# First feed-forward layer: seven products for eight in 1792 of 2816 rows of the down projection, and other places for the weight-quarter loads

## The chip, the cores and the metric

The kernel runs on one core of a Trainium2 chip. TensorE (PE) multiplies, VectorE (DVE) and ScalarE (ACT) evacuate, round and add, GpSimd (POOL) does small work and issues the DMAs that add into their destination, and SyncE (SP) issues the other DMAs. The metric is the device time of one execution in microseconds.

## The reference, cut to what matters

Two transformer-like blocks follow each other on x of 512 tokens by 1024 channels. The change lies in the feed-forward layer of the first block; a part of it touches that of the second.

```python
D_FF = 2816
# first block
h = rms_norm(x, pre_ffn_norm[l])
f = (jax.nn.silu(h @ w_gate[l]) * (h @ w_up[l])) @ w_down[l]   # w_down: 2816 x 1024
x = x + rms_norm(f, post_ffn_norm[l])
...
# end of the second block
h = rmsnorm(x, norm_ffn[i])
x = x + jnp.square(jax.nn.relu(h @ w_up[i])) @ w_down[i]       # w_down_2: 4096 x 1024
return rmsnorm(x, norm_final)
```

## The kernel before, in words

**Arithmetic.** Every float32 matrix product is done as three products of rounded parts: each operand is split into a high part (`hi`, `hH`, `aH`, `fH`: an ACT copy into a rounded type) and the rest (`lo`, `hL`, `aL`, `fL`: a DVE subtraction), and PE adds high by high, high by low and low by high in one PSUM bank. A matmul has 128 rows of weights and moves 512 columns (256 in the blocks of kind `half`).

**Units, slots, blocks.** Weights come in units of 256 rows by 512 columns (512 KB). SP loads a unit into one of three buffers `raw` (`load_unit`), ACT rounds it into one of six `hi` buffers, DVE writes the rest into `lo` (`split_weights` on both). The list `BLOCKS` fixes the order: for the first feed-forward layer `gu0` to `gu10` (each makes 256 of the 2816 hidden columns, gate and up) with the down projection in three pieces between them: `dn00`, `dn01` after `gu2` (768 rows), `dn10`, `dn11` after `gu6` (1024 rows), `dn20`, `dn21` after `gu10` (1024 rows). PE's program is a list of numbered slots, mostly of 6 matmuls of 512 columns or 12 of 256. Every engine's program is written slot by slot from the same tables (`CONV_AT` for conversions, `TR_AT` for transposes, `DONE_AT` for evacuations, `FS_*_AT` for the seven products), but no engine waits for a slot: it runs through its own list in order and waits on semaphores alone. What stands ahead in an engine's list therefore holds up everything behind it.

**Start of a layer.** `gu0` and `up0` (first block of the second layer) are of kind `half`: 16 slots, first for tokens 0 to 255, then from slot 8 on for tokens 256 to 511. Meanwhile the normalised tiles of the later tokens are still transposed: PE turns tile `i` (into banks `s`, semaphore `s_ntr`), ACT rounds it (`norm_round`, `hH<-s`), DVE makes the rest (`norm_rest`, `hL<-s`, semaphore `s_nlo`). In `gu0` the last two turns (i = 14 and 15) stand in slots 6 and 7, ACT's roundings of them in its slots 7 and 8, and PE's slot 8 waits until `s_nlo` shows 15. ACT's conversion of the second unit of `gu1` stands in slot 6, ahead of both roundings. In `up0` the last turn (the 44th) stands in slot 5. The conversions of the four units of the next block stand in slots 2, 6, 10 and 14, and the evacuations of the block itself (ACT, then DVE) behind them, in slots 15 and 16; the next block's first slot waits for the first of these evacuations.

**Seven products.** The second layer's down projection already goes in four rounds `fs0` to `fs3`, each with 1024 rows, as a 2 by 2 by 2 product of parts in seven products for eight. Per round SP loads one quarter each into the buffers `a`, `b`, `c`, `d` (`wq`, for `a` the two buffers `hn`), two DMAs of 512 KB for each (`load_quarter`), and POOL adds further quarters to them by adding DMAs (`later_quarters`), so that the sums of weights cost no engine. The sums of the hidden part are DVE's (`sum_hidden`), and each is rounded and split (`round_hidden`, `rest_hidden`). The 28 slots of a round take 14 conversions of weights, 14 evacuations, 8 roundings and 8 rests. `WQ_BEFORE` says ahead of which unit SP issues a quarter: for `fs0` ahead of its own first four units, which need no `raw` load, so behind all loads of `up1`. The quarters of `fs0` wait for `s_ntr` 44, since they overwrite `hn`.

```python
def load_quarter(f, i):                                        # L800, before
    w, j, n = (("d", 1, 1), ("b", 0, 1), ("a", 0, 0), ("c", 1, 0))[i]
    u0 = BLK["fs0"].u0 if f == 0 else BLK[f"fs{f - 1}"].u0
    for x in range(2):
        if f == 0:
            o.wait_ge(s_ntr, 44)
```

Of the kernel before, what the change touches and what calls it, by code (L numbers as in the profile page):

```python
# [15 lines left out]
S = 512  # L16
# [82 lines left out]
def blocks():  # L99
# [89 lines left out]
def conversions():  # L189
# [239 lines left out]
FS_D_AT = when([s0(f"fs{f}") + s for f in range(NFF2) for s in (-30, -24, -22, -2, -1, 2)])  # L429
FS_S_AT = when([s0(f"fs{f}") + s for f in range(NFF2) for s in (-14, 1, 2, 3)])  # L430
# [43 lines left out]
def build(nc, A, out, scr):  # L474
    ctx = ExitStack()
    with ctx:
# [37 lines left out]
        s_fhi, s_flo, HID = s_ahi, s_alo, 2 * sum(nb for _, nb in FF1)  # L514
# [32 lines left out]
        s_wd, WD_FROM = s_os, 64  # L547
# [119 lines left out]
        WQ = [x[:, :].rearrange("p (k n) -> p k n", k=2) for x in HN] + [sb(f"wq{i}", [128, 2, 512], c=P8)[:, :, :] for i in range(6)]  # L667
# [5 lines left out]
        def fa(i, j):  # L673

            return FA[j - 1][:, :, 256 * i - 256:256 * i]


        def landed(f, w, n):
# [3 lines left out]
            return s_wd[WQ_I[w] // 2], WD_FROM + 32 * ((WQ_PER[w] - 1) * f + n - 1)  # L682
# [4 lines left out]
        def sync_program(e):  # L687
# [6 lines left out]
            def load_gain(i):  # L694
# [9 lines left out]
                if i in (5, 7):  # L704
                    o.wait_ge(s_xup, {5: 8, 7: 16}[i])
# [18 lines left out]
            def load_unit(b, u):  # L724
# [75 lines left out]
            def load_quarter(f, i):  # L800

                w, j, n = (("d", 1, 1), ("b", 0, 1), ("a", 0, 0), ("c", 1, 0))[i]
                u0 = BLK["fs0"].u0 if f == 0 else BLK[f"fs{f - 1}"].u0
                for x in range(2):
                    if f == 0:

# [4 lines left out]
                    e.dma_start(WQ[WQ_I[w] + x], rows(A["w_down_2"][0], 4 * f + 2 * j + x, 512 * n, 512 * n + 512)).then_inc(s_wq[WQ_I[w] // 2], 16)  # L811
# [34 lines left out]
        def scalar_program(e):  # L846
# [48 lines left out]
            def split_weights(j):  # L895

                f = [f for f in range(NFF2) if 0 <= j - BLK[f"fs{f}"].u0 < 14]
                if f:
# [53 lines left out]
            def evacuate(b, i):  # L952
# [19 lines left out]
                elif n[:2] == "gu":  # L972
                    g = int(n[2:])

                    if g:
# [4 lines left out]
                elif n[:2] == "dn":  # L980

                    o.wait_ge(s_xup, 8)
                    h = int(n[3])
                    e.activation(Y[:, i, 512 * h:512 * h + 512], bank[:, :], ACT.Copy).then_inc(s_eva, 1)
                elif n[:2] == "ex":
                    j = int(n[2])

                    o.wait_ge(s_os[i], 16 * j)
# [30 lines left out]
                elif n[:2] == "up":  # L1019
                    k = int(n[2])  # L1020

                    if k >= 2:
                        o.wait_ge(s_flo, HID + 8 * (k // 2))
                    e.activation(FA[k % 2][:, i, :], bank[:, :], ACT.Relu).then_inc(s_rl, 1)

            def round_products(b, i):

                n = b.name
                if n[:2] == "gu" and i >= 2:
                    g = int(n[2:])  # L1030
                    o.wait_ge(s_evd, EVACUATED[b.e0 + i][1])
                    c = [b0 for b0, _ in FF1 if b0 <= g][-1]

                    if c:
                        x = BLK[f"dn{[b0 for b0, _ in FF1].index(c) - 1}1"]
                        o.wait_ge(s_bank, x.e0 + 4)
                    e.activation(aH[:, 2 * (g - c) + i - 2, :], SG[i - 2][:, :], ACT.Copy).then_inc(s_ahi, 1)
# [127 lines left out]
            def convolutions(g):  # L1165
                for i in CV_AT.get(g, ()):
# [4 lines left out]
                    o.wait_ge(s_xsv, 16)  # L1171
# [1464 lines left out]
```

## Time and profile before

| | us |
|---|---|
| median of 3 runs | 1813.27 (1813.20 to 1813.41) |
| the profiled execution | 1813.32 |
| its span | 1811.5 |
| PE busy | 1776.8 (98%) |
| DVE busy | 1114.1 (62%) |
| ACT busy | 834.3 (46%) |
| POOL busy | 336.4 (19%) |

The span is the execution without 1.8 us at its ends. PE's busy time is that of its records, which overlap: a matmul of 512 columns is shown with 0.39 us, while the next one starts 0.23 us later. How much PE really gets done is seen better from the number of matmuls in a stretch. Times inside the program are microseconds from the start of the span. The first layer's part that is changed runs from about 222 to 585 us, the second feed-forward layer from about 1474 us to the end.

### The profile page before, as it was taken

How to read it: one execution, taken by the hardware profiler on the slowest of the kernel's cores; microseconds unless marked ns; L12 is line 12 of the kernel's file. 1: busy time of each engine (PE TensorE's matmuls, PEld its weight loads, DVE VectorE, ACT ScalarE, POOL GpSimd, SP SyncE). 2: the span in 40 equal slices, each digit the busy share in tenths (PEclk: the TensorE clock that was granted, in tenths of full speed). 3: DMA queues.
4: the chain of work that ended last, by engine and by line, in shares of the span. 5: the costliest groups of instructions: out<-in, count | busy, mean ns of one | idle time of the engine just before them, and what ended most of it. 6: DMA issues, size and time to landing. Idle time of an engine off the chain costs nothing.

```text
span 1811.5 us, 24680 instructions
## 1 busy us (share of the span) xinstructions
PE 1776.8 (98%) x9586; PEld 1449.5 (80%) x9586; DVE 1114.1 (62%) x1763; ACT 834.3 (46%) x1593; POOL 336.4 (19%) x404
## 2 busy tenths in 40 slices
PE   7999999999999999999999999999999999999998
PEld 7767898888888877878878787767788998888886
DVE  7556643233345787887768746677556357574847
ACT  5346532222224555554555644554434445352535
POOL 1403000000000046254462640000020012112120
PEclk9999999999999999999999999999999999999999
DMA  7212333332322453352433444233443248849482
GB/s 256 72 58 63 101 110 116 93 93 93 94 93 75 152 143 128 119 149 97 160 131 123 142 147 164 86 105 118 139 151 130 69 148 189 236 101 259 117 206 70
DMA packets 140419, 230.85 MB, mean 127 GB/s; under 512 B 27264, under 2 KB 59456, under 8 KB 139664
## 3 DMA queue, kind: packets, MB, share of 16 engines
q1 hardware_dynamic: 118944, 166.70, 29.0%
q0 software_dynamic: 20496, 60.10, 12.5%
q10 hardware_dynamic: 864, 2.49, 0.3%
q8 instruction: 76, 1.25, 0.3%
q14 instruction: 39, 0.32, 0.1%
HBM read 216.54 MB, written 12.71 MB: 127 GB/s over the span
## 4 chain that ended last, share of the span: by engine, by line
PE 80%; DVE 11%; ACT 3%; DMA 3%; issue 2%; POOL 1%; SPq 0%; DVEq 0%; ACTq 0%; POOLq 0%
PE m L2135 14%; PE m L2137 13%; PE m L2136 13%; PE m L2146 6%; PE m L2148 6%; PE m L2147 6%; PE s L2298 4%; DVE lo L1396 3%; DMA raw<-in_w_up_dram 2%; PE m L2245 2%; PE m L2244 2%; PE m L2243 2%; PE s L2294 1%; PE m L2270 1%; PE m L2272 1%
## 5 line engine op out<-in xcount | busy, mean ns | idle before, releaser
L2135 PE MATMUL m<-hH,hi 128*128 128x512 f32 (+1 forms) x1392 | 529.4, 380 | 3.2 <-DVE hL L1426 1.8
L2137 PE MATMUL m<-hH,lo 128*128 128x512 f32 (+1 forms) x1392 | 509.1, 366 | 0.0
L2136 PE MATMUL m<-hL,hi 128*128 128x512 f32 (+1 forms) x1392 | 508.3, 365 | 0.0
L1396 DVE TENSOR_TENSOR lo<-raw,hi 128x1024 fp32r<-128x1024 f32 x267 | 335.8, 1269 | 189.7 <-ACT hi L916 189.4
L916 ACT ACTIVATE hi<-raw 128x1024 fp32r<-128x1024 f32 x267 | 276.1, 1050 | 200.8 <-DMA raw<-in_w_up_dram 52.9
L2135 PEld LDWEIGHTS m<-hH,hi 128*128 128x128 f32 x1392 | 262.6, 189 | 47.7 <-DVE hL L1426 2.4
L2137 PEld LDWEIGHTS m<-hH,lo 128*128 128x128 f32 x1392 | 262.4, 189 | 43.4
L2136 PEld LDWEIGHTS m<-hL,hi 128*128 128x128 f32 x1392 | 262.9, 189 | 39.0
L2146 PE MATMUL m<-hi,hH 128*128 128x512 f32 (+1 forms) x320 | 133.8, 418 | 1.6 <-DVE lo L1396 1.6
L2148 PE MATMUL m<-hi,hL 128*128 128x512 f32 (+1 forms) x320 | 122.5, 383 | 0.0
L2147 PE MATMUL m<-lo,hH 128*128 128x512 f32 (+1 forms) x320 | 122.4, 382 | 0.0
L1463 DVE TENSOR_TENSOR sg<-sg,m 128x512 f32<-128x512 f32 x44 | 29.8, 685 | 116.1 <-ACT sg L979 111.3
L2243 PE MATMUL m<-hi,fH 128*128 128x512 f32 x224 | 87.1, 389 | 0.0
L2244 PE MATMUL m<-lo,fH 128*128 128x512 f32 x224 | 87.1, 389 | 0.0
L2245 PE MATMUL m<-hi,fL 128*128 128x512 f32 x224 | 87.1, 389 | 0.0
L1226 ACT ACTIVATE X<-hn,BIAS 128x128 f32<-128x128 f32 x256 | 80.7, 391 | 4.4 <-POOL hn L2015 4.3
L2077 POOL DMA_DIRECT2D scr_x_dram<-X x1 | 0.5, 542 | 414.1 <-DVE X L1447 414.1
L2060 POOL DMA_DIRECT2D wq<-in_w_down_dram x32 | 39.2, 1645 | 184.2 <-DMA wq<-in_w_down_dram 111.2
L2146 PEld LDWEIGHTS m<-hi,hH 128*128 128x128 f32 x320 | 60.5, 189 | 13.6 <-DVE lo L1396 2.1
L2148 PEld LDWEIGHTS m<-hi,hL 128*128 128x128 f32 x320 | 60.5, 189 | 12.3
L905 ACT ACTIVATE hi<-wq 128x1024 fp32r<-128x1024 f32 x40 | 42.1, 1054 | 58.2 <-PE m L2137 40.6
L2146 PE MATMUL m<-hi,aH 128*128 128x512 f32 x176 | 68.9, 391 | 0.0
(330 smaller groups left out, 3032.6 us busy)
## 6 DMA issues: line engine op xcount, KB each, us to landing
raw<-in_w_in_dram SPq DMA_DIRECT2D x72, 512.0 KB, 3.6
wq<-in_w_down_dram POOLq DMA_DIRECT2D x40, 512.0 KB, 10.0
hn<-scr_cs_dram POOLq DMA_DIRECT2D x32, 512.0 KB, 4.1
raw<-in_w_up_dram SPq DMA_DIRECT2D x32, 512.0 KB, 5.7
wq<-in_w_down_dram SPq DMA_DIRECT2D x24, 512.0 KB, 7.7
raw<-in_w_gate_dram SPq DMA_DIRECT2D x44, 256.0 KB, 2.8
raw<-in_w_up_dram SPq DMA_DIRECT2D x44, 256.0 KB, 3.1
raw<-in_w_down_dram SPq DMA_DIRECT2D x22, 512.0 KB, 4.2
```

The source lines that it names most:

```text
L916: e.activation(d, r, ACT.Copy).then_inc(s_hi, 1)
L1226: x = e.activation(to[:, h % 2, k], HN[h % 2][:, 512 * d + 128 * c:512 * d + 128 * c + 128], ACT.Exp, bias=BIAS[:, c, 32 * d + h:32 * d + ...
L1396: e.tensor_tensor(d, r, h.bitcast(F32), ALU.subtract).then_inc(s_lo, 1)
L2135: e.matmul(bank, wh[:, kk, c], h[:, k, q], start=k == 0, stop=False)
L2136: e.matmul(bank, wh[:, kk, c], l[:, k, q], start=False, stop=False)
L2137: x = e.matmul(bank, wl[:, kk, c], h[:, k, q], start=False, stop=k == kt - 1)
L2146: e.matmul(bank, h[:, k, q], wh[:, kk, c], start=k == 0, stop=False)
L2147: e.matmul(bank, h[:, k, q], wl[:, kk, c], start=False, stop=False)
L2148: x = e.matmul(bank, l[:, k, q], wh[:, kk, c], start=False, stop=k == kt - 1)
L2243: e.matmul(m[:, :], fH[n % 4][:, k, q], wh[:, kk, :], start=k == 0 and p in FS_FRESH, stop=False, skip_group_check=True)
L2244: e.matmul(m[:, :], fH[n % 4][:, k, q], wl[:, kk, :], start=False, stop=False, skip_group_check=True)
L2245: y = e.matmul(m[:, :], fL[n % 4][:, k, q], wh[:, kk, :], start=False, stop=k == 3, skip_group_check=True)
```

## The change

- The down projection's first 768 rows (`ds0`, after `gu2`) and the next 1024 (`ds1`, after `gu6`) are done in seven products, as in the second layer; the last 1024 rows stay as they were (`dn20`, `dn21`). In `ds0` each half of the rows has 3 blocks of 128, so every second slot has 3 matmuls instead of 6. `dn00`, `dn01`, `dn10`, `dn11` are gone. The number of slots stays 1106; the units grow from 323 to 337.
- DVE writes the product of gate and up for `gu0` to `gu6` into `fa1` buffers; ACT and DVE don't split it there any more. The products of `ds0`, `ds1` are evacuated by DVE into `Y`, by a multiplication by 1 or -1 the first time.
- The buffers for the quarters are `hn` (a), the four rows of `X` (b, c), `gain0` and a new buffer `wqf` (d). So `X` is saved to `scr_x` by a 2 MB DMA of POOL when its first update is done, and brought back near the end of `ds1`. Two gain vectors are loaded later (ahead of `gu8` instead of `gu2`).
- SP issues the quarters of `ds0` ahead of units of `gu1` and `gu2`, those of `ds1` ahead of units of `gu4`, `gu5`. They wait for `s_ntr` 16, `s_hn` 16 and `s_mlo` 8, b and c also for the saved `X`.
- For the second layer the quarters of `fs0` now stand ahead of the second, third and fourth unit of `up1` and of the first of `fs0`; those of `fs1` to `fs3` are spread over more units too. POOL's adding DMAs have new slots.

```diff
-FF1 = [(0, 3), (3, 4), (7, 4)]
+FF1 = 7
 NFF2 = 4
+SEVEN = ["ds0", "ds1"] + [f"fs{f}" for f in range(NFF2)]
...
+    for b in range(11):
+        add(f"gu{b}", "fm" if b else "half", 4, "dddd")
+        if b in (2, 6):
+            add(f"ds{b // 4}", "fs", 14, "d" * 14)
+    for h in range(2):
+        add(f"dn2{h}", "tmt" if h else "tm", 4, "dddd")
...
-WQ_BEFORE = {BLK[f"up{2 * f}"].u0 + u: (f, i) for f in range(NFF2) for i, u in enumerate((3, 4, 5, 6) if f else (8, 9, 10, 11))}
+SEVEN_K = [3, 4] + [4] * NFF2
+SEVEN_ROW = [0, 768] + [1024 * f for f in range(NFF2)]
+WQ_AFTER = [[("gu1", 1), ("gu2", 0), ("gu1", 3), ("gu2", 2)], [("gu4", 0), ("gu4", 2), ("gu5", 0), ("gu5", 2)], [("up1", 1), ("up1", 2), ("up1", 3), ("fs0", 0)]]
...
+def unit_tiles(f, x):
+    return SEVEN_K[f] - 2 if x else 2
...
             def load_quarter(f, i):
                 w, j, n = (("d", 1, 1), ("b", 0, 1), ("a", 0, 0), ("c", 1, 0))[i]
...
                     if f == 0:
+                        o.wait_ge(s_ntr, 16)
+                        o.wait_ge(s_hn, 16)
+                        o.wait_ge(s_mlo, 8)
+                        if w in ("b", "c"):
+                            o.wait_ge(s_xsv, 16)
+                    elif f == 2:
                         o.wait_ge(s_ntr, 44)
...
+                    d = s[:, :]
+                    if i >= 2 and g < FF1:
...
+                        d = FA1[k // SEVEN_K[c]][:, k % SEVEN_K[c], :]
+                    e.tensor_tensor(d, s[:, :], bank[:, :], ALU.mult).then_inc(s_evd, 1)
...
+                    if first and not f:
+                        e.tensor_scalar(x, bank[:, :], -1.0 if i // 2 in FS_MINUS else 1.0, None, ALU.mult).then_inc(s_evd, 1)
...
+                if g == s0("gu1") + 2:
+                    o.wait_ge(s_xup, 8)
+                    e.dma_start(scr["x"], X[:, :, :].rearrange("p t d -> p (t d)")).then_inc(s_xsv, 16)
+                if g == s0("gu7") + 2:
+                    o.wait_ge(s_lo, BLK["ds1"].u0 + 12)
+                    e.dma_start(X[:, :, :].rearrange("p t d -> p (t d)"), scr["x"]).then_inc(s_xbk, 16)
...
-                    for kk in range(2):
+                    for kk in range(unit_tiles(n // 7, x)):
```

**SP's list at `gu1`, before.** The rows are the loads of the first, second and third unit of `gu1` (each a gate half and an up half), then those of the fourth with a gain vector:

```order
L741 DMA raw1<-in_w_up_dram 128x2x256
L740 DMA raw2<-in_w_gate_dram 128x2x256 [waits s_lo]
L741 DMA raw2<-in_w_up_dram 128x2x256
L740 DMA raw0<-in_w_gate_dram 128x2x256 [waits s_lo]
L741 DMA raw0<-in_w_up_dram 128x2x256
L740 DMA raw1<-in_w_gate_dram 128x2x256 [waits s_lo]
L741 DMA raw1<-in_w_up_dram 128x2x256
L740 DMA raw2<-in_w_gate_dram 128x2x256 [waits s_lo]
L741 DMA raw2<-in_w_up_dram 128x2x256
L722 DMA gain1<-in_post_ffn_norm_dram 128x1024 [waits s_xup]
```

The same place now; `raw2` is the first unit of `gu1`, `raw0` the second:

```order
L786 DMA raw2<-in_w_gate_dram 128x2x256 [waits s_lo]
L787 DMA raw2<-in_w_up_dram 128x2x256
L864 DMA gain0<-in_w_down_dram 128x2x512 [waits s_mlo,s_hn,s_ntr]
L864 DMA wqf<-in_w_down_dram 128x512
L786 DMA raw0<-in_w_gate_dram 128x2x256 [waits s_lo]
L787 DMA raw0<-in_w_up_dram 128x2x256
L786 DMA raw1<-in_w_gate_dram 128x2x256 [waits s_lo]
L787 DMA raw1<-in_w_up_dram 128x2x256
L864 DMA hn0<-in_w_down_dram 128x2x512
L864 DMA hn1<-in_w_down_dram 128x512
L786 DMA raw2<-in_w_gate_dram 128x2x256 [waits s_lo]
L787 DMA raw2<-in_w_up_dram 128x2x256
```

Quarter d now stands, with its three waits, between the first and the second unit of `gu1`, and quarter a ahead of the fourth.

**ACT's list in `gu0`, now** (the same instructions in the same order as before). `hi2` is the first unit of `gu1`, `hi3` the second, `hH<-s2` and `hH<-s3` are the roundings of tiles 14 and 15:

```order
L969 ACTIVATE hi2<-raw2 128x1024 [waits s_unit,s_raw2]
L1003 ACTIVATE hH<-s0 128x4x128 [waits s_ntr]
L1003 ACTIVATE hH<-s1 128x4x128 [waits s_ntr]
L969 ACTIVATE hi3<-raw0 128x1024 [waits s_raw0]
L1003 ACTIVATE hH<-s2 128x4x128 [waits s_ntr]
L1003 ACTIVATE hH<-s3 128x4x128 [waits s_ntr]
```

Nothing moved here: `hi3` still stands ahead of the last two roundings; what moved is the load that it waits for.

**SP's list at `up1`, before.** `raw2`, `raw0`, `raw1` ahead of `wq4` are the second to fourth unit of `up1`:

```order
L798 DMA raw1<-in_w_up_2_dram 128x2x512 [waits s_lo]
L798 DMA raw2<-in_w_up_2_dram 128x2x512 [waits s_lo]
L798 DMA raw0<-in_w_up_2_dram 128x2x512 [waits s_lo]
L798 DMA raw1<-in_w_up_2_dram 128x2x512 [waits s_lo]
L798 DMA raw2<-in_w_up_2_dram 128x2x512 [waits s_lo]
L811 DMA wq4<-in_w_down_2_dram 128x2x512 [waits s_ntr]
L811 DMA wq5<-in_w_down_2_dram 128x2x512
L811 DMA wq0<-in_w_down_2_dram 128x2x512
L811 DMA wq1<-in_w_down_2_dram 128x2x512
L811 DMA hn0<-in_w_down_2_dram 128x2x512
L811 DMA hn1<-in_w_down_2_dram 128x2x512
L811 DMA wq2<-in_w_down_2_dram 128x2x512
```

The same place now, from the first unit of `up1` on:

```order
L844 DMA raw1<-in_w_up_2_dram 128x2x512 [waits s_lo]
L864 DMA wq4<-in_w_down_2_dram 128x2x512 [waits s_ntr]
L864 DMA wq5<-in_w_down_2_dram 128x2x512
L844 DMA raw2<-in_w_up_2_dram 128x2x512 [waits s_lo]
L864 DMA wq0<-in_w_down_2_dram 128x2x512
L864 DMA wq1<-in_w_down_2_dram 128x2x512
L844 DMA raw0<-in_w_up_2_dram 128x2x512 [waits s_lo]
L864 DMA hn0<-in_w_down_2_dram 128x2x512
L864 DMA hn1<-in_w_down_2_dram 128x2x512
L844 DMA raw1<-in_w_up_2_dram 128x2x512 [waits s_lo]
L864 DMA wq2<-in_w_down_2_dram 128x2x512
L864 DMA wq3<-in_w_down_2_dram 128x2x512
```

The quarters moved ahead of three of the four loads of `up1`; counted from `wq4`, these are the third, sixth and ninth DMA.

## Rows read from the trace of the kernel before

**Rows 1.** Stretches: busy time and count of each engine, granted clock, DMA.
```profile
core 0: us, PE busy (x) PEld busy (x) DVE busy (x) ACT busy (x) POOL busy (x), PEclk, DMA share, GB/s
...
400.00:500.00 100.00, 100.00 (x443) 82.81 (x442) 36.13 (x42) 24.43 (x29) 0.00 (x0) 1.00 0.28 88
```

**Rows 2.** The same columns, one round of seven products (`fs1`).
```profile
1601.40:1639.50 38.10, 38.10 (x170) 31.55 (x169) 34.26 (x38) 19.84 (x21) 4.15 (x4) 1.00 0.42 106
```

**Rows 3.** SP in order of time, around `gu0`: start, duration, instruction.
```profile
221.36 0.37 SPq L740 DMA_DIRECT2D raw<-in_w_gate_dram  x1
221.77 0.76 SPq L741 DMA_DIRECT2D raw<-in_w_up_dram  x1
```

**Rows 4.** ACT in order of time, in `gu0`.
```profile
229.40 1.05 ACT L916 ACTIVATE hi<-raw 128x1024 fp32r<-128x1024 f32 x1
232.84 0.60 ACT L950 ACTIVATE hH<-s 128x512 fp32r<-128x512 f32 x1 [2.39 <-PE s L2298]
234.72 0.60 ACT L950 ACTIVATE hH<-s 128x512 fp32r<-128x512 f32 x1 [1.28 <-PE s L2298]
```

**Rows 5.** PE (first two) and DVE (last) in order of time, in `gu0`.
```profile
234.08 0.60 PE L2298 MATMUL s<-CST,hn 128*128 128x128 f32 x4
234.44 0.36 PE L2135 MATMUL m<-hH,hi 128*128 128x256 f32 x1
...
233.47 0.69 DVE L1426 TENSOR_TENSOR hL<-s,hH 128x512 fp32r<-128x512 f32 x1 [0.41 <-ACT hH L950]
```

**Rows 6.** SP in order of time, at `up0`.
```profile
1474.39 7.13 SPq L798 DMA_DIRECT2D raw<-in_w_up_dram  x3
1482.35 1.91 SPq L811 DMA_DIRECT2D wq<-in_w_down_dram  x4
```

**Rows 7.** Landing times of quarter DMAs issued together: the 1st; 2nd and 3rd; 7th and 8th.
```profile
DMA to landing us min/median/max: 5.1/5.1/5.1
...
DMA to landing us min/median/max: 6.7/7.0/7.3
...
DMA to landing us min/median/max: 11.7/13.4/15.0
```

**Rows 8.** SP (first) and POOL: issues of the last two quarters, first adding DMAs.
```profile
1486.28 1.54 SPq L811 DMA_DIRECT2D wq<-in_w_down_dram  x2
...
1489.77 2.54 POOL L2060 DMA_DIRECT2D wq<-in_w_down_dram  x2 [11.73 <-DMA wq<-in_w_down_dram]
```

**Rows 9.** ACT, DVE and PE in order of time, where `up0` ends and `up1` begins.
```profile
1492.49 1.06 ACT L916 ACTIVATE hi<-raw 128x1024 fp32r<-128x1024 f32 x1 [1.82 <-PE m L2137]
1496.03 2.76 ACT L1024 ACTIVATE fa<-m 128x512 f32<-128x512 f32 x4 [2.48 <-PE m L2137]
...
1496.73 1.41 DVE L1504 TENSOR_TENSOR fa<-fa,m 128x512 f32<-128x512 f32 x2 [4.80 <-PE m L2137]
...
1497.99 0.40 PE L2135 MATMUL m<-hH,hi 128*128 128x512 f32 x1
```

**Rows 10.** Landing time of two plain loads of the same queue, at `gu0` (gate and up).
```profile
DMA to landing us min/median/max: 2.7/2.7/2.7
...
DMA to landing us min/median/max: 3.0/3.2/3.3
```

**Rows 11.** Landing time of the 2 MB store of `X`, at `bc0`.
```profile
DMA to landing us min/median/max: 7.7/7.7/7.7
```

**Rows 12.** Stretches around the longest pause of PE; columns as in rows 1.
```profile
655.00:660.00 5.00, 2.29 (x23) 1.60 (x23) 4.90 (x5) 4.11 (x10) 4.04 (x6) 1.00 0.72 197
660.00:665.00 5.00, 5.00 (x18) 3.94 (x16) 4.89 (x6) 1.44 (x4) 0.56 (x1) 0.66 0.76 198
```

**Rows 13.** DVE in order of time in `fs1`: a sum, a rest, an evacuation.
```profile
1604.27 1.22 DVE L1551 SCALAR_TENSOR_TENSOR gain<-fa 128x1024 f32<-128x1024 f32 x1
...
1610.14 1.22 DVE L1535 TENSOR_TENSOR fL<-gain,fH 128x1024 fp32r<-128x1024 f32 x1
1611.27 0.68 DVE L1517 TENSOR_TENSOR X<-m,X 128x512 f32<-128x512 f32 x1
```

More of the change, by code:

```diff
@@ L513, in build @@
         s_gs, s_ahi, s_alo, s_rl = (sem(f"s_{n}") for n in ("gs", "ahi", "alo", "rl"))
-        s_fhi, s_flo, HID = s_ahi, s_alo, 2 * sum(nb for _, nb in FF1)
+        s_fhi, s_flo = s_ahi, s_alo
         s_cwt, s_cw, s_cid, s_tanh, s_silu = (sem(f"s_{n}") for n in ("cwt", "cw", "cid", "tanh", "silu"))
@@ L666, in build, with fa, sums, part @@
         fL = [sb(f"fL{i}", [128, 4, 256], F32R, c=P8) for i in range(4)]
-        WQ = [x[:, :].rearrange("p (k n) -> p k n", k=2) for x in HN] + [sb(f"wq{i}", [128, 2, 512], c=P8)[:, :, :] for i in range(6)]
+        WQ2 = [x[:, :].rearrange("p (k n) -> p k n", k=2) for x in HN] + [sb(f"wq{i}", [128, 2, 512], c=P8)[:, :, :] for i in range(6)]
         P8.close()
         FS2 = G[1][:, :].rearrange("p (k t) -> p k t", k=4)
-        def fa(i, j):
-            return FA[j - 1][:, :, 256 * i - 256:256 * i]
+        def fa(f, i, j):
+            return (FA if f >= 2 else FA1)[j - 1][:, 0:SEVEN_K[f], 256 * i - 256:256 * i]
+        def sums(f):
+            return FS2[:, 0:SEVEN_K[f], :]
+        def part(f, p):
+            return [fa(f, 1, 1), fa(f, 1, 2), sums(f), fa(f, 1, 1), fa(f, 2, 1), fa(f, 1, 2), fa(f, 2, 2)][p]
+        def split_part(n):
+            if n < 14:
+                return tuple(x[:, 2 * (n % 4):2 * (n % 4) + 2, :].rearrange("p a (b c) -> p (a b) c", b=2) for x in (aH, aL))
+            return fH[n % 4], fL[n % 4]
+        def wq(f, w, x):
+            return (WQ2 if f >= 2 else WQ0)[WQ_I[w] + x][:, 0:unit_tiles(f, x), :]
+        def quarter(f, j, c, x):
+            w = A["w_down_2"][0] if f >= 2 else A["w_down"][0]
+            r0 = SEVEN_ROW[f] + 128 * (SEVEN_K[f] * j + 2 * x)
+            return w[r0:r0 + 128 * unit_tiles(f, x), 512 * c:512 * c + 512].rearrange("(k p) n -> p k n", p=128)
         def landed(f, w, n):
@@ L703, in load_gain @@
                     o.wait_ge(s_sn, 4)
-                if i in (5, 7):
-                    o.wait_ge(s_xup, {5: 8, 7: 16}[i])
+                if i == 5:
+                    o.wait_ge(s_xup, 8)
+                    o.wait_ge(s_flo, rests(1) + 8)
+                if i == 6:
+                    o.wait_ge(s_lo, BLK["ds1"].u0 + 14)
+                if i == 7:
+                    o.wait_ge(s_xup, 16)
                 if i in (9, 10):
@@ L1028, in round_products @@
                 n = b.name
-                if n[:2] == "gu" and i >= 2:
+                if n[:2] == "gu" and int(n[2:]) >= FF1 and i >= 2:
                     g = int(n[2:])
                     o.wait_ge(s_evd, EVACUATED[b.e0 + i][1])
[L1032 to L1037, printed above, removed]
+                    o.wait_ge(s_bank, BLK["ds1"].e0 + 14)
+                    e.activation(aH[:, 2 * (g - FF1) + i - 2, :], SG[i - 2][:, :], ACT.Copy).then_inc(s_ahi, 1)
             def round_hidden(g):
@@ L1411, in norm_scale @@
                     o.wait_ge(s_ntr, 2 * n - 2)
+                if 8 <= n < 12:
+                    o.wait_ge(s_lo, BLK["ds1"].u0 + 8)
                 if n >= 12:
@@ L2233, in block @@
                     p, t, x = s // 4, s // 2 % 2, s % 2
-                    n, i, j = 7 * int(b.name[2]) + p, s // 2, b.u0 + 2 * p + x
-                    o.wait_ge(s_flo, HID + 8 * (n // 7) + (x + 2 if p == 1 else FS_LAST[p] + 1))
+                    n, i, j = 7 * SEVEN.index(b.name) + p, s // 2, b.u0 + 2 * p + x
+                    o.wait_ge(s_flo, rests(n // 7) + (x + 2 if p == 1 else FS_LAST[p] + 1))
+                    hh, hl = split_part(n)
+                    last = SEVEN_K[n // 7] - 1
                     wh, wl = weights(j)
```

179 lines of the change are left out of this document (95 added, 84 removed).

## The prediction

> **What bounds the kernel now.** The page first: PE is busy for 98% of the span, DVE for 62%. So I looked for what PE does per 100 us, in the view of stretches: 443 matmuls of 512 columns start in 100 us of the first layer [rows 1], which is 0.226 us each. In the round `fs1`, the pattern that the change copies, the stretch holds 170 matmul records (168 of its own and two cut at the ends) in 38.1 us, again 0.226 us each, and DVE is busy for 34.3 of the 38.1 us [rows 2]. So the seven products don't slow PE, though DVE has little left there. PE is the bound in both layers; what it is spared counts in full, and every wait that reaches it as well. Then I read SP, ACT, DVE and PE in order of time at the two places where SP's list changes: `gu0` [rows 3 to 5] and `up0` [rows 6 to 9].
>
> **What is removed.** Before: 14 blocks of 128 rows by 4 token tiles by 2 halves by 3 = 336 matmuls. Now: `ds0` has 7 products by 2 tiles by 3 blocks by 3 = 126, `ds1` 7 by 2 by 4 by 3 = 168, together 294. 42 matmuls go, at 0.226 us each [rows 1]: **-9.5 us**. The weights are loaded beside the matmuls as before. Bounds: -9.0 to -9.7, since nothing else of PE changes in these blocks.
>
> **The products beside DVE.** In `ds0` PE needs 126 by 0.226 = 28.5 us. DVE has from its start on, by its list: 14 evacuations and the last product of `gu2` at 0.60 (an operation of 0.68 overlaps its neighbour by 0.08), 7 rests and 3 sums at 0.87 (three quarters of the 1.22 of 1024 elements, less the overlap), 9 conversions of quarters, 5 of them short ones (0.60), 4 long (1.14), and 4 of `gu3` at 1.14: 9.0 + 8.7 + 3.0 + 4.6 + 4.6 = 29.9 us [rows 13]. That is 1.4 us more than PE, but the last two operations on this list are wanted only in `gu3`. The tightest point is the third product, at 8.2 us in `ds0`: by the same costs its rest is done at 7.2, a lead of 1 us. In `fs1` it is done 9.9 us after the start (1611.4 to 1601.4) and wanted at 10.9, the same lead, and PE loses nothing [rows 2, 13]. `ds1` has the sizes of `fs1`. I take **0** for both, bounds 0 and +4 (every product late by some tenths). The 14 additional conversions, the DMAs of POOL (its list is empty in this layer) and the two 2 MB copies of `X` lie beside PE. The store lands 7.7 us after its issue [rows 11], begins at about 226 and so is over before the quarters start.
>
> **Stall A, in `gu0`.** SP issued the load of the second unit of `gu1` at 221.36 [rows 3]; ACT converted it at 229.40, ahead of the roundings of tiles 14 and 15 at 232.84 and 234.72 [rows 4]. Now quarter d stands ahead of this load and waits for `s_ntr` 16, the last turn of PE, which starts at 234.08 and is seen by ACT at 234.72 [rows 4, 5]. So SP stands still from 221.4 to 234.7. Then it issues two DMAs for d (0.75 MB) and the two halves of the unit (0.5 MB). When do they land? Of quarters issued together the first lands after 5.1 us, the second 6.7 after its issue, the third 7.3 [rows 7], with 0.48 us between issues [rows 6]; counted from the first issue 5.1, 7.2 and 8.3 us for 0.5, 1.0 and 1.5 MB. For 1.25 MB that is 7.7 us: 242.4. Lower bound: the unit lands as if alone, 3.2 us after its own issue at 236.2 [rows 10], at 239.4; upper bound 8.3 us and 2 us more for other traffic, 245. I take the middle one, as a burst like that of rows 7 stands there. Then ACT converts (1.05), rounds tile 14 (0.6), DVE makes the rest (0.69) [rows 4, 5]: 244.7. PE's slot 8 needs this rest. Slot 7 begins at 234.44 and has 12 matmuls at 0.12, so slot 8 would begin at 235.9; before, the rest was there at 234.2 (233.47 and 0.69) [rows 5]. PE stands still for 244.7 - 235.9 = **8.8 us**, bounds 5.8 and 11.4. No other engine can give this back: PE was the bound, and tiles 14 and 15 wait behind the conversion whatever else is ready. This is the cover that is gone: between load and conversion lay 8 us, and the wait takes 13.
>
> **Stall B, at `up1`.** The same wait, `s_ntr` 44, now stands in front of the second unit of `up1`, and the quarters between its units. The roundings of the last turn are ahead of the conversion here, so `up0` itself is not held up. But the fourth unit, whose load was issued long before the quarters [rows 6], is now the ninth of a burst that begins at 1482.35. The seventh and eighth of that burst land at 1498.0 and 1502.2 (11.7 and 15.0 us after issues at 1486.3 and 1487.2) [rows 7, 8], the last ones slowed by the adding DMAs from 1489.77 on [rows 8]. A ninth at the pace of the earlier ones, 1 to 2 us apart, lands at about 1503.7; bounds 1497.8 (the pace of the first ones throughout) and 1506.4 (the 4.2 us between the last two once more). ACT converts it in slot 14, ahead of the evacuations of `up0`; before at 1492.49, and these at 1496.03 [rows 9]. Then: 1.06 for the conversion, 0.6 for the first evacuation, 0.69 for DVE's: 1506.0. PE's first slot of `up1`, at 1497.99 before [rows 9], waits for that: **8.0 us**, bounds 2 and 10.7.
>
> The Trainium skill, "DMA: Bandwidth & Descriptors", section "Queues, rings and completion order", says that an SDMA engine takes one queue's descriptors in ring order, while completion is not FIFO for one issuing engine. By the ring order the ninth load can't pass the eight ahead of it, and stall B stands; the trace agrees so far, as the landings of rows 7 rise with the order of issue. If completion in another order decided, it would be the second rival's case at `up1`; no row shows one.
>
> **The clock.** PE had one longer pause, 655 to 660, busy for 2.29 of 5 us; in the next 5 us its granted clock was 0.66 in the mean [rows 12], so some of it ran at 1.2 GHz instead of 2.4. That cost 0.34 by 5 = 1.7 us. Both stalls are longer than that pause: **+1.7** each, bounds 0 and 2.
>
> **Other waits.** The quarters of `ds1`, `fs1` to `fs3` wait for conversions (`s_lo`) that are done by then or some slots ahead of the next need. The late loads of `up2` have 13 slots to their use. The wait for the saved `X` (quarter b) is met by 235. I take 0.
>
> **Sum** against the profiled execution, 1813.3 (0.05 above the median): 1813.3 - 9.5 + 8.8 + 1.7 + 8.0 + 1.7 = **1824.0 us**. Its own range by the bounds, not all at one end: 1817 to 1829.
>
> **Rivals.**
> 1. *Neither stall reaches PE*: the plain gain, 1803.8. For it: PE's waits are short at both places now, and only 8 us of one load's lateness must vanish. Against it: SP's wait is for an event at 234.7, 5.3 us after the conversion's start before, and two DMAs and a landing come on top; it would need the unit to land by 233.6. At `up1` the ninth load would have to land by 1495.6, ahead of the seventh in rows 7. Chance 0.14.
> 2. *One stall only*, most likely A, with B hidden because the units of `up1` pass the quarters: 1813.3 - 9.5 + 8.8 + 1.7 = 1814.3; with B only 1813.5. Or both stalls near their lower bounds: 1813.3 - 9.5 + 5.8 + 2 + 1.7 = 1813.3. Chance 0.23.
> 3. *Both stalls, and DVE too slow in the products*: the 29.9 us of DVE beside 28.5 of PE decide as soon as the rest of the third product is over 1 us later than worked out; then each of the 7 products waits some tenths, +2 to +4, with 1 or 2 more in `ds1`: 1827 to 1830. For it: DVE has no gap for the first 28 us. Against: `fs1` at the same lead loses nothing. Chance 0.11.
>
> The forecast has 0.52. The two stalls end the gain on the other side: the point from which the change is slower is a sum of both, clock included, of 9.5 us, and I count 20.2.
>
> **Numbers.** This kernel's measurement tells 0.2%, 3.6 us, from no change. Faster (under 1809.7): rival 1 and a little of rival 2, 0.15. Within 0.2% (to 1816.9): rival 2 and the lowest end of the forecast, 0.24. Slower: 0.61. The range must leave out no more than 0.2: rival 1 lies at 1803.8 with 0.14, so it begins at 1812 and ends at 1829.
>
> **What would show it.** A: in the profile after, SP issues quarter d at about 234.7; ACT's conversion of the second unit of `gu1` starts at 242 instead of 229.4; PE waits some 9 us for `hL` in `gu0`, the longest wait of the program; the granted clock is under 1 after it. B: at `up1` PE waits 8 us for DVE's `fa` products, ACT's conversion ahead of the evacuations starts after 1500 plus the shift. The gain: `ds0` takes 28.5 us, `ds1` 38. Wrong would be: PE's longest wait in `gu0` stays under 2 us (rival 1), or waits of PE inside `ds0` or `ds1` (rival 3).

## The result, and the profile after

The changed kernel takes **1831.0 us** (median of 4, 1829.2 to 1835.6), the kernel before 1813.2 (1812.2 to 1813.4): the ratio is 1.0103, with a 95% interval of 1.0084 to 1.0122. It is slower by 1.0%, as forecast, but by 17.7 us instead of 10.7, and its time lies 2 us above the range of the prediction.

Its profiled execution took 1831.26 us, with a span of 1829.0. The page, in its first part (busy time, share of the span, instructions):

```profile
PE 1774.1 (97%) x9544; PEld 1446.0 (79%) x9544; DVE 1149.3 (63%) x1807; ACT 846.4 (46%) x1601; POOL 363.7 (20%) x430
```

PE has 42 matmuls fewer and the program is longer, so PE stands still or runs at a lower clock somewhere. PE's waits by releaser (us in total, times, longest) name the two places of the forecast:

```profile
PE m L2202 <- DVE fa L1561: 11.8, 3, 7.4
...
PE m L2202 <- DVE hL L1474: 9.7, 3, 8.1
```

The longest of the first is stall B, the longest of the second stall A. But the first shows three waits, and 4.4 us beside the longest: those the prediction did not have. (Neither is the longest wait of the program: before its first matmul PE waits 8.6 us for DVE's first norm, in both kernels.) The four long waits in PE's order of time, then SP, ACT and DVE at the first of them (stall A, to be read beside [rows 3 to 5]):

```profile
244.09 0.58 PE L2202 MATMUL m<-hH,hi 128*128 128x256 f32 x1 [8.08 <-DVE hL L1474]
...
1505.57 0.80 PE L2202 MATMUL m<-hH,hi 128*128 128x512 f32 x1 [7.37 <-DVE fa L1561]
...
1677.89 0.74 PE L2202 MATMUL m<-hH,hi 128*128 128x512 f32 x1 [2.46 <-DVE fa L1561]
...
1763.62 0.50 PE L2202 MATMUL m<-hH,hi 128*128 128x512 f32 x1 [1.94 <-DVE fa L1561]
```

```profile
234.60 0.37 SPq L864 DMA_DIRECT2D gain<-in_w_down_dram  x1
235.01 0.47 SPq L864 DMA_DIRECT2D wqf<-in_w_down_dram  x1
235.53 0.43 SPq L786 DMA_DIRECT2D raw<-in_w_gate_dram  x1
236.00 0.47 SPq L787 DMA_DIRECT2D raw<-in_w_up_dram  x1
...
241.76 1.06 ACT L969 ACTIVATE hi<-raw 128x1024 fp32r<-128x1024 f32 x1 [12.36 <-DMA raw<-in_w_up_dram]
242.73 1.07 ACT L1003 ACTIVATE hH<-s 128x512 fp32r<-128x512 f32 x2
...
243.34 0.69 DVE L1474 TENSOR_TENSOR hL<-s,hH 128x512 fp32r<-128x512 f32 x1 [10.37 <-ACT hH L1003]
```

SP issued nothing in the 26 us from 208.6 to 234.60 (before, it issued the unit at 221.36), then the two DMAs of quarter d, then that unit of `gu1` [rows 3]. ACT stood in front of this unit's conversion for 12.36 us, with the two roundings behind it.

Stall B, where `up0` ends: SP's list, and ACT's (beside [rows 6, 8, 9]).

```profile
1482.39 0.88 SPq L864 DMA_DIRECT2D wq<-in_w_down_dram  x2
...
1486.63 0.90 SPq L844 DMA_DIRECT2D raw<-in_w_up_dram  x1
...
1503.18 1.06 ACT L969 ACTIVATE hi<-raw 128x1024 fp32r<-128x1024 f32 x1 [8.07 <-DMA raw<-in_w_up_dram]
1504.14 2.04 ACT L1074 ACTIVATE fa<-m 128x512 f32<-128x512 f32 x4
```

The fourth unit of `up1` is the ninth 512 KB in the burst and lands some 16 us after its issue. The granted clock behind both stalls (stretches: us, busy time and count of PE, PEld, DVE, ACT, POOL, clock, DMA share, GB/s):

```profile
244.00:248.00 4.00, 3.91 (x19) 3.92 (x20) 1.76 (x3) 0.00 (x0) 0.00 (x0) 0.53 1.09 246
...
1504.00:1508.00 4.00, 2.43 (x6) 1.95 (x7) 3.17 (x5) 4.00 (x7) 3.33 (x3) 0.50 1.06 235
1508.00:1512.00 4.00, 4.00 (x14) 3.15 (x13) 3.96 (x5) 1.13 (x2) 0.62 (x1) 0.66 1.13 207
```

Where 4 us at full speed hold some 36 matmuls of 256 columns, the first stretch has 19: PE ran at 1.2 GHz for nearly all of it. The loss is 3.91 by 0.47 = 1.8 us behind A and 2.43 by 0.50 plus 4.00 by 0.34 = 2.6 us behind B.

The seven products themselves run as hoped. `ds0`, then `ds1`, as stretches (beside [rows 2]):

```profile
301.40:329.90 28.50, 28.50 (x127) 23.62 (x126) 27.49 (x36) 15.61 (x20) 1.37 (x2) 1.00 0.26 56
417.30:455.40 38.10, 38.10 (x170) 31.55 (x169) 34.37 (x38) 18.72 (x19) 2.76 (x3) 1.00 0.47 124
```

PE has no gap in either, though DVE is busy for 27.49 of the 28.50 us of `ds0`.

The time after, summed from the trace: -9.5 for the matmuls; A 8.1 and 1.8 of clock; B 7.4 and 2.6; 0.5 where `gu3` follows `ds0` (332.02, a wait for one of DVE's evacuations into `Y`); and in the second layer's later blocks 0.9 where `up4` begins (1652.02), 2.5 where `up5` begins with 1.7 of clock, 1.9 where `up7` begins. That is +17.9, and the two profiled executions differ by 17.9; waits of some tenths that differ elsewhere are left out. The clock behind the pause of 2.5 us:

```profile
1677.89:1681.00 3.11, 3.11 (x8) 2.46 (x9) 3.08 (x4) 2.59 (x3) 0.00 (x0) 0.51 0.25 59
1681.00:1682.00 1.00, 1.00 (x5) 0.82 (x4) 1.00 (x2) 0.00 (x0) 0.00 (x0) 0.80 1.07 389
```

### The profile page after: what moved, and what is told of

Read it like the earlier page. It is cut to its first block, busy times and chain, and to the rows that moved or that the text cites. A ratio compares the mean times of both kernels' runs of the same rounds, so it can differ in the third digit from the quotient of the medians.

```text
span 1829.0 us, 24697 instructions
## 1 busy us (share of the span) xinstructions
PE 1774.1 (97%) x9544; PEld 1446.0 (79%) x9544; DVE 1149.3 (63%) x1807; ACT 846.4 (46%) x1601; POOL 363.7 (20%) x430
## 4 chain that ended last, share of the span: by engine, by line
PE 74%; DVE 13%; DMA 5%; ACT 3%; issue 2%; POOL 1%; SPq 0%; DVEq 0%; ACTq 0%; POOLq 0%
PE m L2202 13%; PE m L2204 13%; PE m L2203 13%; PE m L2213 5%; DMA raw<-in_w_up_dram 5%; PE m L2215 4%; PE m L2214 4%; PE s L2367 3%; DVE lo L1442 3%; PE m L2312 2%; PE m L2313 2%; PE m L2314 2%; PE m L2339 1%; PE s L2363 1%; DVE lo L1436 1%
## 5 line engine op out<-in xcount | busy, mean ns | idle before, releaser
L1442 DVE TENSOR_TENSOR lo<-raw,hi 128x1024 fp32r<-128x1024 f32 (+1 forms) x253 | 319.2, 1270 | 182.6 <-ACT hi L969 181.9
L969 ACT ACTIVATE hi<-raw 128x1024 fp32r<-128x1024 f32 (+1 forms) x253 | 262.2, 1050 | 230.2 <-DMA raw<-in_w_up_dram 139.2
L2213 PEld LDWEIGHTS m<-hi,hH 128*128 128x128 f32 x320 | 60.5, 189 | 14.1 <-DVE lo L1442 2.5
L1521 DVE TENSOR_TENSOR sg<-sg,m 128x512 f32<-128x512 f32 x30 | 20.5, 686 | 80.9 <-ACT sg L1034 76.0
L2214 PEld LDWEIGHTS m<-lo,hH 128*128 128x128 f32 x320 | 60.7, 190 | 9.2
L1319 ACT ACTIVATE SC<-SC,ST 128x256 f32<-128x256 f32 (+1 forms) x64 | 35.5, 555 | 53.7 <-DVE ST L1898 53.7
```

The source lines that it names most:

```text
L969: e.activation(d, r, ACT.Copy).then_inc(s_hi, 1)
L1442: e.tensor_tensor(d, r, h.bitcast(F32), ALU.subtract).then_inc(s_lo, 1)
L2213: e.matmul(bank, h[:, k, q], wh[:, kk, c], start=k == 0, stop=False)
L2214: e.matmul(bank, h[:, k, q], wl[:, kk, c], start=False, stop=False)
```

## The experiments

**My theory** was the prediction's: SP's wait in front of a quarter holds the unit loads behind it, and the conversions of these units stand in ACT's list ahead of what PE wants next. **The rivals**: the quarters' traffic, not the wait, makes the units late; the later pauses come from POOL's adding DMAs at new slots (`FS_D_AT`), not from SP's list; and the order of ACT's list alone decides, so that a conversion placed later would mend it. In every edit, `WQ_AFTER` says ahead of which unit SP issues the four quarters of `ds0`, `ds1`, `fs0` and so on.

### Quarters of ds0 late (A undone)

```diff
-WQ_AFTER = [[("gu1", 1), ("gu2", 0), ("gu1", 3), ("gu2", 2)], ...
+WQ_AFTER = [[("gu2", 0), ("gu2", 1), ("gu2", 2), ("gu2", 3)], ...
```

> The quarters of ds0 stand in SyncE's list ahead of gu2's four units instead of among gu1's and gu2's; all else is the changed kernel. Theory 1 (the wait of SyncE for the norm holds the raw loads, whose conversion stands in ScalarE's list ahead of the norm's own copies): the pause of 8.1 us at the start of gu0's next products and the fall of the clock behind it (1.9 us) go, 1831.0 -> 1821 us, with no pause over 1 us before 250 us. Theory 2 (the pause comes from the traffic: the same bytes are only in flight at another time and the weights land late all the same): the pause moves to gu1 or gu2 and the time stays within 3 us of 1831. Theory 3 (the quarters now land after ds0's first products want them): a pause in front of ds0's first products, at about 255 to 300 us, of several us, 1824 to 1831 us.

Measured: **1820.6 us** (5 runs, 1817.4 to 1821.5), 10.4 below the changed kernel, and the pause in `gu0` is gone. Of the second unit of `gu1`, gate and up are issued on time and its conversion is done before the last two roundings, as before the change:

```profile
222.85 0.37 SPq L786 DMA_DIRECT2D raw<-in_w_gate_dram  x1
...
230.85 1.06 ACT L969 ACTIVATE hi<-raw 128x1024 fp32r<-128x1024 f32 x1
234.30 0.60 ACT L1003 ACTIVATE hH<-s 128x512 fp32r<-128x512 f32 x1 [2.39 <-PE s L2367]
```

The 8.1 and 1.8 us read from the trace of after add up to 9.9; the 10.4 measured agree with that within the spread of the runs. The quarters, now landing later, are still there when `ds0` wants them. Theories 2 and 3 fall.

### Quarters of fs0 late (B undone)

```diff
-..., [("up1", 1), ("up1", 2), ("up1", 3), ("fs0", 0)]]
+..., [("fs0", 0), ("fs0", 1), ("fs0", 2), ("fs0", 3)]]
```

> The quarters of fs0 stand where the kernel before had them (in front of fs0's units), all else is the changed kernel. Theory 1: the pause of 7.4 us in up1 and the fall of the clock behind it (2.6 us) go: 1831.0 -> 1821 us. Theory 2 (the second layer lost time for another reason, the new slots of GpSimd's adding DMAs for one): the time stays at 1829 to 1833 us, with a pause of about the same length in up1.

Measured: **1819.3 us** (7 runs, 1816.8 to 1823.4), 11.7 below the changed kernel, 1.7 more than expected. The pause in `up1` is gone; those in `up4`, `up5` and `up7` stay, at 0.5, 1.6 and 1.8 us. POOL's slots are the changed kernel's here, so theory 2 falls for B.

### The conversion behind the roundings (the order of ACT's list)

```diff
+        if j == BLK["gu1"].u0 + 1:
+            s = max(s, BLK["gu0"].s0 + 8)
```

> The quarters stand where the changed kernel has them and SyncE waits as long, but the conversion of gu1's second unit stands two places later in ScalarE's and VectorE's lists, behind the rounding of the norm's last columns. Theory 1 (order of the lists): the pause of 8.1 us goes though SyncE is held as long as before, 1831.0 -> 1821 us, or to 1823 if gu1's weights are then a little late. Theory 2 (traffic, or SyncE's wait as such): the load lands as late and the time stays at 1829 to 1833 us, the pause now in front of gu1's first products.

Measured: **1830.2 us** (4 runs, 1828.7 to 1833.8), no gain. My theory 1 missed here, and the trace says why. ACT (first four) and PE:

```profile
234.72 0.60 ACT L1005 ACTIVATE hH<-s 128x512 fp32r<-128x512 f32 x1 [3.34 <-PE s L2369]
236.59 0.60 ACT L1005 ACTIVATE hH<-s 128x512 fp32r<-128x512 f32 x1 [1.28 <-PE s L2369]
243.38 1.06 ACT L971 ACTIVATE hi<-raw 128x1024 fp32r<-128x1024 f32 x1 [6.20 <-DMA raw<-in_w_up_dram]
...
252.92 1.06 ACT L971 ACTIVATE hi<-raw 128x1024 fp32r<-128x1024 f32 x1 [6.24 <-DMA raw<-in_w_up_dram]
...
256.73 0.80 PE L2204 MATMUL m<-hH,hi 128*128 128x512 f32 x1 [7.22 <-DVE sg L1523]
```

The roundings are on time and `gu0` runs through. But the second to fourth units of `gu1` are all late, the last one by far, and its conversion stands ahead of the evacuations of `gu0`. The pause is 7.2 us at 256.7 instead of 8.1 at 244.1. So the order of the lists decides only where the lateness comes out; the lateness itself is in the loads. Rival 1 of the prediction counted the lateness of one load alone; those behind it are late too.

### The waits kept, the quarters taken from there (hold or traffic)

The quarters of `ds0` and `fs0` are issued late, but SP still makes their waits early:

```diff
+                    if b.u0 + u == BLK["gu1"].u0 + 1:
+                        o.wait_ge(s_ntr, 16)
+                        o.wait_ge(s_hn, 16)
+                        o.wait_ge(s_mlo, 8)
+                    if b.u0 + u == BLK["up1"].u0 + 1:
+                        o.wait_ge(s_ntr, 44)
```

> The DMAs of the quarters of ds0 and fs0 stand late, in front of gu2's and fs0's units, but SyncE still makes their two waits (for the norm, and for the transposes of the second layer's norm) where the changed kernel makes them, at gu1's and up1's second units. So SyncE is held as in the changed kernel, and the quarters' traffic is gone from there. Theory 1 (the hold delays the weights behind it): both pauses are still there, 5 to 8 us each, with the clock 1825 to 1831 us. Theory 2 (the quarters' traffic makes the weights land late, the hold does little): 1809 us, as with both quarters late. In between, some 1817 us, each would have its half.

### The same without the waits (A and B undone)

Both `WQ_AFTER` edits above together.

> The quarters of ds0 and of fs0 both late, each as in the run that had it alone, the rest as the changed kernel. If the two pauses are independent, their gains add: 1831.0 - 10.4 - 11.7 = 1808.9 us, below the kernel before (1813.4). If they are not (a pause gone in one place comes back further on), 1813 to 1819 us.

Measured: with the waits **1817.4 us** (10 runs, 1815.1 to 1819.9), without them **1811.9** (10 runs, 1808.1 to 1813.9; the ratio to the kernel before is 0.9988, 0.9979 to 0.9997). The second is 3 us above the 1808.9 at which the two single gains would add up, and 1 us under the range of the other expectation. The runs of each kernel spread over 4 to 7 us, so whether a little of the two gains is shared stays open; most of them adds.

The waits alone cost 5.6 us, against 19.1 for waits and early quarters together. At `gu0` (SP, ACT, PE, in this order):

```profile
234.67 0.37 SPq L786 DMA_DIRECT2D raw<-in_w_gate_dram  x1
235.08 0.47 SPq L787 DMA_DIRECT2D raw<-in_w_up_dram  x1
...
238.15 1.06 ACT L975 ACTIVATE hi<-raw 128x1024 fp32r<-128x1024 f32 x1 [8.67 <-DMA raw<-in_w_up_dram]
...
240.47 0.39 PE L2208 MATMUL m<-hH,hi 128*128 128x256 f32 x1 [4.40 <-DVE hL L1480]
```

SP is held until the same 234.7, but the unit is the first thing out of the queue and is there 3.1 us after the issue of its second half, against 5.8 in the changed kernel (236.00 to 241.76). The pause is 4.4 us instead of 8.1: a little over half of stall A is SP's wait, the rest are the 0.75 MB of quarter d ahead of the unit (0.9 us of issue and 2.7 of landing; at the 289 GB/s that the core moves from 235 to 244, the 0.79 million bytes of the quarter take 2.7 us).

At `up1` there is no pause at all (PE's only two waits of this kind are 2.2 us at `up5` and 1.9 at `up7`). SP and ACT:

```profile
1480.32 1.39 SPq L844 DMA_DIRECT2D raw<-in_w_up_dram  x3
1481.75 2.60 SPq L864 DMA_DIRECT2D wq<-in_w_down_dram  x4
...
1490.46 1.06 ACT L975 ACTIVATE hi<-raw 128x1024 fp32r<-128x1024 f32 x1 [1.82 <-PE m L2210]
1494.00 2.76 ACT L1080 ACTIVATE fa<-m 128x512 f32<-128x512 f32 x4 [2.48 <-PE m L2210]
```

The last three units of `up1` wait just as long for their issue, and the quarters follow 1.4 us behind them, so the traffic is as thick as in the changed kernel: 352 GB/s from 1481 to 1497, against 296 from 1482.4 to 1503.2. Only the order in the queue differs: units first, quarters behind. ACT's conversions wait for PE now, not for a DMA. So stall B is neither SP's wait nor the traffic as such. It is six quarter DMAs standing ahead of the last unit in one queue, eight DMAs of 512 KB in all with two units.

### The same places in the kernel before

Only the places of `fs0` to `fs3` are taken over into the kernel before; its first layer and POOL's slots are untouched.

```diff
-WQ_BEFORE = {...: (f, i) for f in range(NFF2) for i, u in enumerate((3, 4, 5, 6) if f else (8, 9, 10, 11))}
+WQ_BEFORE = {...: (f, i) for f in range(NFF2) for i, u in enumerate((2, 4, 5, 7) if f else (5, 6, 7, 8))}
```

> The kernel before, with one thing of the change alone: SyncE's quarters of the second layer at the new places (fs0 to fs3). The first layer is as it was. Theory 1 (these places cost the pauses of up1, up4, up5 and up7): 10.0 us in up1 and 6.7 us in the later blocks, so 1813.2 -> 1830 us. Theory 2 (only up1 is due to the places, the later pauses to other edits, such as GpSimd's adding DMAs at new slots): 1823 us. Theory 3 (the places cost nothing): 1813 us.

Measured: **1825.9 us** (4 runs, 1823.4 to 1829.2), 12.5 above the kernel before. PE's long waits:

```profile
1505.65 0.79 PE L2135 MATMUL m<-hH,hi 128*128 128x512 f32 x1 [8.46 <-DVE fa L1504]
...
1676.31 0.50 PE L2135 MATMUL m<-hH,hi 128*128 128x512 f32 x1 [0.73 <-DVE fa L1504]
1760.69 0.50 PE L2135 MATMUL m<-hH,hi 128*128 128x512 f32 x1 [1.96 <-DVE fa L1504]
```

Stall B and the pauses of `up5` and `up7` are all there with POOL's adding DMAs at their old slots. So SP's places make them. The median is 4 us under theory 1. For the most part that is `up5`: its pause is 0.7 us and not 2.5, with no fall of the clock behind it. The unit that decides there lands 13.9 us after its issue (1660.02 to 1673.92), against 15.3 in the changed kernel (1660.17 to 1675.50); why it lands sooner, with the same places, the runs don't show.

### Quarters of fs1 to fs3 late (C undone)

```diff
-WQ_AFTER += [[(f"up{2 * f}", 2), (f"up{2 * f + 1}", 0), (f"up{2 * f + 1}", 1), (f"up{2 * f + 1}", 3)] ...
+WQ_AFTER += [[(f"up{2 * f}", 3), (f"up{2 * f + 1}", 0), (f"up{2 * f + 1}", 1), (f"up{2 * f + 1}", 2)] ...
```

> Only the quarters of fs1 to fs3 where the kernel before had them, all else the changed kernel. Theory 1: the pauses of 0.9, 2.5 and 1.9 us in up4, up5 and up7 go, with 1.4 us of clock: 1831.0 -> 1824.3 to 1826 us. Theory 2 (these pauses come from the adding DMAs): they stay, 1831 us.

Measured: **1826.2 us** (4 runs, 1822.7 to 1828.0), 4.8 below the changed kernel, just above theory 1's range. The pauses of `up4` and `up5` are gone, that of `up7` is down from 1.94 to 0.43 us.

### All three undone

All three `WQ_AFTER` edits. What stays of the change is the products of `ds0` and `ds1`, the quarters of `ds1`, POOL's slots and the buffers.

> The quarters of ds0, fs0 and fs1 to fs3 all late (those of the second layer where the kernel before had them), the products, ds1's quarters and all else as the changed kernel. Theory 1 (the later pauses of up4, up5 and up7, 3.8 to 5.3 us and up to 1.4 us of clock, come from the places of fs1 to fs3's quarters): 1804 us, within 1.5 us of 1813.4 less the 9.5 us of the 42 matmuls. Theory 2 (they come from GpSimd's adding DMAs at their new slots): the time stays at 1809 us, as with the first two alone.

Measured: **1804.2 us** (5 runs, 1803.5 to 1804.7); the ratio to the kernel before is 0.9951 (0.9937 to 0.9964). This version beats both kernels. The kernel before had 1813.6 in these runs, so 9.4 us are gained where 42 matmuls by 0.226 are 9.5 (by the interval, 6.5 to 11.4). The trace has one wait more than that of before, 0.6 us at 322.10, where `gu3` follows `ds0`; beside it the products cost PE nothing that shows. Three stretches of 100 us, of the changed kernel and then of this one:

```profile
200.00:300.00 100.00, 91.38 (x500) 79.29 (x499) 46.26 (x65) 36.75 (x70) 10.49 (x11) 0.97 0.56 159
1500.00:1600.00 100.00, 94.43 (x406) 78.00 (x407) 61.70 (x66) 41.19 (x47) 21.75 (x19) 0.95 0.78 200
1600.00:1700.00 100.00, 96.61 (x418) 79.23 (x417) 56.99 (x62) 39.21 (x45) 15.69 (x15) 0.98 0.66 165
```

```profile
200.00:300.00 100.00, 99.43 (x544) 85.82 (x543) 55.35 (x78) 42.40 (x78) 12.63 (x13) 1.00 0.62 167
1500.00:1600.00 100.00, 100.00 (x443) 82.81 (x442) 63.53 (x69) 43.40 (x50) 18.49 (x17) 1.00 0.76 187
1600.00:1700.00 100.00, 99.92 (x441) 82.27 (x440) 69.58 (x76) 44.04 (x49) 13.69 (x12) 1.00 0.61 153
```

With the same instructions PE is busy throughout again, at full clock, with 544, 443 and 441 matmuls in place of 500, 406 and 418.

### Which quarter of fs1 to fs3

On top of the last kernel, one of the two moved quarters each is put where the change has it. First the first quarter, then the last:

```diff
-WQ_AFTER += [[(f"up{2 * f}", 3), ...
+WQ_AFTER += [[(f"up{2 * f}", 2), ...
```

> Base is the kernel with all of the quarters late (1804.15 us). Of fs1 to fs3 the first quarter alone is moved ahead by one unit, to where the changed kernel has it (the third unit of up2, up4, up6). Theory 1 (this quarter waits for the seven products' last halves, so SyncE is held with the third and fourth units of up2, up4, up6 behind it, and their late conversions stand in front of the evacuations): most of the pauses of up4, up5 and up7, 4 to 8 us: 1808 to 1812 us. Theory 2 (the last quarter, further on, is the one that matters): 1804 us.

```diff
-... (f"up{2 * f + 1}", 1), (f"up{2 * f + 1}", 2)] ...
+... (f"up{2 * f + 1}", 1), (f"up{2 * f + 1}", 3)] ...
```

> Base as before (1804.15 us). Of fs1 to fs3 the last quarter alone is moved back by one unit, from the third to the fourth unit of up3, up5 and up7, as the changed kernel has it. Theory 1 (only the first quarter's place matters; this move puts one more load of weights ahead of the quarter): 1804 us. Theory 2: the quarter lands late for the products that want it, or the fourth unit's load is the one that is late in up5 and up7: 1808 to 1812 us.

Measured: **1809.3 us** with the first quarter early (10 runs, 1804.6 to 1811.6), **1805.1** with the last one late (4 runs, 1803.9 to 1806.0; the difference of 1.0 us to 1804.2 can't be told from none). So it is the first quarter, which has two units of its own block and all of the next block behind it: 5.2 of the 7.7 us that lie between 1811.9 and 1804.2. The profiled execution of the first shows less than its median: PE waits 0.9 and 0.4 us in `up5`, and its 1806.4 us are 2.9 below the median. With this spread of 7 us between runs I take the place as shown and the size only roughly; no trace of a run near the median was kept.

## Why the prediction was right or wrong

**The matmuls, -9.5: right.** 9.4 measured where nothing else is in the way.

**The products beside DVE, 0: right for the products, 0.5 short behind them.** PE doesn't wait inside `ds0` or `ds1`, and the rest of the third product is done 7.2 us after the start of `ds0` (308.6), as counted. The last operations of DVE's list, said to be wanted only in `gu3`, are wanted there: PE waits 0.5 us for one of them at 332.02, within the bound of 4. Rival 3, with 2 to 4 us in the products, didn't happen; that its 1827 to 1830 came nearest to the time was chance.

**Stall A, 8.8 and 1.7: right in mechanism and size.** 8.1 and 1.8 in the trace, 10.4 when undone. SP was held to 234.6 (234.7 worked out), the unit was there at 241.8 (242.4 worked out). The cause is in two parts that the prediction had both put in, the hold (4.4 us of pause) and the quarter ahead in the queue (3.7). Wrong was that a later place for the conversion would help: it was not in the prediction's sum, but in my theory for the experiment.

**Stall B, 8.0 and 1.7: the stall right, its clock too small.** 7.4 us of pause; the unit was there at 1503.2, 1503.7 worked out. The clock cost 2.6, above the bound of 2: it was taken from the stretch 655 to 660 [rows 12], which isn't one longer pause but two short ones, 1.6 us at 655.76 and 1.9 at 659.38, and behind B the clock stayed low for longer. Another slip had no effect on the sum: the fourth unit of `up1` was not issued long before the quarters, but at 1481.15, 1.2 us ahead of them. The Trainium skill, "DMA: Bandwidth & Descriptors", section "Queues, rings and completion order", has an engine take one queue's descriptors in ring order; the runs agree, since the same units and quarters cost 7.4 us with the quarters ahead and nothing with them behind.

**The step that failed is "Other waits", taken as 0.** The prediction asked there only whether the quarters of `fs1` to `fs3` have to wait, and whether the late loads of `up2` are late. It did not take the first quarter of `fs1` to `fs3` through SP's list as it did for `ds0` and `fs0`, though it too was moved ahead of two unit loads. SP around `up4` and ACT at the end of `up4`, in the kernel before and then in the changed one:

```profile
1581.15 1.39 SPq L798 DMA_DIRECT2D raw<-in_w_up_dram  x3
1626.92 3.24 SPq L811 DMA_DIRECT2D wq<-in_w_down_dram  x2
...
1647.40 0.37 SPq L798 DMA_DIRECT2D raw<-in_w_up_dram  x1
...
1661.53 1.06 ACT L916 ACTIVATE hi<-raw 128x1024 fp32r<-128x1024 f32 x1 [2.03 <-DMA raw<-in_w_up_dram]
```

```profile
1637.02 3.24 SPq L864 DMA_DIRECT2D wq<-in_w_down_dram  x2
1640.30 1.69 SPq L844 DMA_DIRECT2D raw<-in_w_up_dram  x2
...
1660.17 0.37 SPq L844 DMA_DIRECT2D raw<-in_w_up_dram  x1
...
1675.50 1.06 ACT L969 ACTIVATE hi<-raw 128x1024 fp32r<-128x1024 f32 x1 [4.87 <-DMA raw<-in_w_up_dram]
1676.46 1.07 ACT L1074 ACTIVATE fa<-m 128x512 f32<-128x512 f32 x2
```

In both kernels the quarter's second half waits for a conversion of the round before, so that its two DMAs spread over 3.2 us. What moved is the third unit of `up4`: it was the last of the three loads from 1581.15, 45 us ahead of the quarter; now it is issued at 1640.30, behind it. ACT and DVE convert the third and fourth unit of `up4` late, an evacuation of `fs1` stands behind the last of these conversions in DVE's list, and PE waits 0.9 us for it at 1652.02. SP reaches the quarter 10.1 us later than before (1637.02 against 1626.92). Counted from there, the first unit of `up5` is converted 2.7 us later (1657.82, before 1645.06), so its buffer comes free and the fourth unit of `up5` is issued 2.7 us later (1660.17, before 1647.40), and it takes 15.3 us to its conversion instead of 14.1. Its conversion stands ahead of the last evacuations of `up4`; it is 3.9 us later in all, and PE waits 2.5 us. A late conversion and a pause go together in other places too, counted in the same way: 1.6 us later and a pause of 0.7 with the new places in the kernel before, 2.0 and 0.9 with only the first quarter early, 2.2 and 1.9 at `up7` of the changed kernel; how large the pause is does not follow from this lateness alone. How full the DMA engines are is not what changed: 269 GB/s from 1630 to 1665 before, 282 from 1640 to 1675 now.

These pauses are 5.3 us in the trace with 1.7 of clock, 4.8 us when undone alone and 7.7 when undone last. Against the 7.0 us by which the time missed the forecast stand 7.0 for these pauses and their clock, 0.9 more clock behind B, 0.1 more behind A and 0.5 at `gu3`, less 1.3 by which the pauses A and B came out shorter. With this one term the forecast would have been 1831.0.

The chances: the case that had 0.52, both stalls, is what happened; nothing pointed to rival 1 or 2.

## What to carry to other kernels

When a load is moved ahead in a queue, take every load behind it through to its use, in each block where this happens, and count the bytes now ahead of it: a unit behind eight others of 512 KB came 16 us after its issue. Put first in the queue what is wanted first; at `up1` the same loads, issued within the same 8 us, cost 7.4 us or nothing by their order alone. An idea and its placing are two things: the seven products gave their 9.4 us as soon as three sets of places were moved back behind the loads that are due first.

## What the runs showed of the hardware

After a stop of 8.1 us PE was granted 0.53 of its clock for the next 4 us, after 7.4 us 0.50 and then 0.66 for 4 us each; after one of 4.4 us it was 0.62 in 3.6 us and 0.91 in the 4 after them, and after one of 2.5 us 0.51 in 3.1 us and 0.80 in the next one. In the 10 us before each of these stops PE had been busy throughout. So even a stop of 2.5 us cost 1.7 us more in clock, about as much as one of 8.1, which I had not expected. Behind the stops of 1.9 us (1763.62), 0.9 (1652.02) and 0.7 (`up5` of the kernel before with the new places) the granted clock was 1.00: there the stop itself was the whole cost.
